# Two joined transformer blocks with routed experts: group and experts chosen in common steps, attention kinds in one sequence, new norms between the stages

## Chip, cores and metric

One core of one Trainium2 chip runs the whole forward pass in one launch. The metric is the device time of one execution in microseconds; less is better. All data is fp32.

## What is computed

Batch 1, 256 tokens of width 1024. The first block also reads 256 context tokens. It modulates and normalises, projects, and mixes in three ways side by side: differential attention (4 heads over context and own tokens), a gated linear scan in two directions ("GLA"), and neighbourhood attention ("na", 4 heads with a bias); then comes the routed feed-forward. The second block has two layers with latent attention, a stick-breaking mixer and pooling, and a routed feed-forward of the same kind.

```python
x = x + mod[2] * (concat([ya, yb, yn]) @ w_out)          # first block
h2 = rms_norm(x, g2) * (1 + mod[4]) + mod[3]
x = x + mod[5] * hier_moe(h2, ...)
x = rms_norm(x, final_g)                                  # between the blocks
# second block, twice:
x = x + mixed(rms_norm(x, norm1_g)) @ w_out
x = x + hier_moe_2(rms_norm(x, norm2_g), ...)
# hier_moe: argmax of 4 groups, the 2 best of the group's 8 experts,
#   gate = softmax(two logits) * softmax(groups)[group]
#   y[token] += gate * (silu(g) * u) @ w_down[expert],  g, u = split(h[token] @ w_up[expert])
```

Each token goes to 2 of 32 experts. An expert of the first block has 6 MB of weights (up 1024 x 1024, down 512 x 1024), one of the second block 3 MB. All the weights of the 32 experts are loaded in each of the three expert stages.

## The kernel before

The five engines run programs of their own that meet at semaphores; `at(name)` in the code counts what an engine has to wait for. `link` puts an operation of VectorE or ScalarE and a wait for its end in one. SyncE issues all weight loads into a ring of slots in SBUF, in a fixed order. A slot is loaded again when it is given back: the up slots by VectorE (`up_used`, after the product of SiLU and up in an expert's last round), the others by TensorE (`piece_used`).

**Attention of the first block.** `attention_pe`, `attention_act` and `attention_dve` work through items, one for each pair of heads (or head with its two maps) and tile of 128 tokens. An item is: scores on TensorE, row maximum on VectorE, exponential on ScalarE, normalisation on VectorE, transposes on TensorE, their copy on ScalarE, and after two items the values on TensorE and their copy (`outputs`) on VectorE. Scores run two items ahead. The kernel calls them twice, with 4 items of "na" and then 8 of "diff"; each call ends before the next begins. The GLA's norm is worked in between: `ones64` sums squares over 64 partitions and spreads the sums, so mean, reciprocal and root are done on 512 columns.

**Residual and norm.** `out_steps_pe` makes 16 matmuls, 8 for each tile of 128 tokens, and `residual_dve` adds a tile to X after its eighth. ScalarE squares each tile with a sum along the row (`squares_act`), VectorE makes the mean and its reciprocal (`rstd_dve`), ScalarE the root (L804), VectorE the scaled tiles (L820), TensorE turns them, VectorE and ScalarE copy with gain and shift.

**Routing** (`route_pe`, `route_dve`). After the logits VectorE chooses the group in five steps (`first_of`: maximum, equal, number, minimum, equal), takes the group's eight logits, chooses the first expert in five steps and the second in five, and writes `chosen` (L950). TensorE meanwhile does sums of zeros to stay busy (L860), then ranks the tokens of each expert with triangular matmuls (L898 to L902). VectorE marks the tokens of the first round (L1248), TensorE gathers their rows.

**Expert rounds** (`experts_pe`, `experts_act`, `experts_dve`). A round serves up to 32 tokens of one expert (of two experts in the second block): turned rows `got`, up matmuls (L1128 or L1137), SiLU (L1218), product (L1285), turned, down matmuls, copy `y_sb` (L1223), combine with the gates into PSUM (L1115). Beside it the next round's rows are gathered. An expert with more tokens has further rounds; their count is read from memory into a register by each engine (`next_extra`). Before the first round VectorE clears `comb` and `y_sb` and works out the gates (`route_gates_dve`), then `each_round` reads the count and starts.

**Joins.** After the first block the combined sum is multiplied by a gate row and added to X, X is normalised with `final_g` and written (L879), then squared and normalised again for the second block's first norm. At the end GpSimd sends X out in one transfer.

**The order of the loads** (`expert_loads`): the first 6 ring loads of a stage go early, others after the mixers, after the residual, and from then on each as its slot comes free.

## Time and profile before

| | us |
|---|---|
| median of the 3 runs shown | 1614.74 |
| lowest and highest of them | 1606.09, 3355.39 |
| the profiled execution | 1603.31 |
| its span | 1601.4 |
| TensorE busy in the span | 1334.5 (83%) |
| VectorE, ScalarE, GpSimd busy | 441.8, 394.3, 44.7 |
| moved by DMA | 479.78 MB, mean 300 GB/s |

The span goes from the first to the last instruction of the profiled execution; some 2 us lie around it. The stages by the trace: to about 200 us modulation and projections, 200 to 292 the mixers, to 333 projection, norm and routing, 333 to 814 the 32 experts of the first block, then a layer to 1197, whose experts begin at 967, and a layer to 1601, whose experts begin at 1343.

### The profile page before, as it was taken

The numbers are of one execution on the slowest core, as the hardware profiler recorded it, in microseconds if no ns is written. First come the engines' busy times: TensorE is split into PE (matmuls) and PEld (weight loads), VectorE is DVE, ScalarE is ACT, GpSimd is POOL, SyncE is SP. The second block draws the span as 40 slices with busy tenths as digits, with TensorE's granted clock in tenths as the row PEclk, the third lists the DMA queues.
The fourth block names the chain that finished last, engine by engine and source line by source line (L and its number), as shares of the span: only waits on it lengthen the run. The fifth ranks groups of instructions, "written<-read, shape, count | busy, mean of one in ns | idle before, by whom it ended". The sixth has DMA issues, their size and how long they took to land.

```text
span 1601.4 us, 31814 instructions
## 1 busy us (share of the span) xinstructions
PE 1334.5 (83%) x12448; PEld 692.8 (43%) x12449; DVE 441.8 (28%) x1332; ACT 394.3 (25%) x766; POOL 44.7 (3%) x68
## 2 busy tenths in 40 slices
PE   4999976988666776699989898987899898999975
PEld 3555443444232332355546543433337544434332
DVE  2004366432111121122233533111122534221212
ACT  2101235122111121122223322222132322222212
POOL 2000210000000000000000000000000000000000
PEclk9999989999899999999999999999899999999987
DMA  9959302769999999989773286999992344689994
GB/s 365 376 208 286 101 9 92 264 240 410 410 410 410 409 410 410 410 357 410 307 288 147 91 309 242 418 417 417 419 381 96 142 147 182 240 321 418 418 417 181
DMA packets 120161, 479.78 MB, mean 300 GB/s; under 512 B 9185, under 2 KB 19774, under 8 KB 103406
## 3 DMA queue, kind: packets, MB, share of 16 engines
q1 hardware_dynamic: 116352, 468.61, 74.4%
q0 software_dynamic: 2848, 8.86, 1.8%
q10 hardware_dynamic: 910, 1.59, 0.3%
q8 instruction: 37, 0.61, 0.2%
q14 instruction: 14, 0.11, 0.0%
HBM read 477.05 MB, written 1.97 MB: 299 GB/s over the span
## 4 chain that ended last, share of the span: by engine, by line
PE 57%; SPq 19%; DMA 9%; DVE 7%; issue 4%; ACT 2%; ACTq 0%; DVEq 0%; POOL 0%; PEldq 0%
SPq L512 19%; PE psum L1137 6%; PE psum L1857 6%; DMA store<-in_w_up 6%; PE psum L761 5%; PE psum L1115 5%; PE psum L1088 5%; PE psum L1128 5%; PE psum L1148 3%; PE psum L1155 2%; PE psum L1853 2%; DMA store<-in_w_expert_up 2%; PE psum L1402 2%; PE psum L1390 2%; PE psum L1435 1%
## 5 line engine op out<-in xcount | busy, mean ns | idle before, releaser
L1128 PE MATMUL psum<-store 128*32 128x256 f32 x2624 | 172.5, 403 | 71.8 <-DMA store<-in_w_expert_up 70.6
L1137 PE MATMUL psum<-store 128*32 128x256 f32 x2432 | 156.4, 414 | 25.1 <-DMA store<-in_w_up 23.1
L1285 DVE TENSOR_TENSOR store<-store,psum 128x128 f32<-128x128 f32 x79 | 22.7, 288 | 528.1 <-ACT store L1218 527.0
L1128 PEld LDWEIGHTS psum<-store 128*32 128x32 f32 x2624 | 78.1, 113 | 150.5 <-DMA store<-in_w_expert_up 99.8
L1088 PE MATMUL psum<-xn,store 128*32 128x256 f32 (+1 forms) x992 | 126.8, 478 | 5.7 <-DVE store L1248 5.7
L1115 PE MATMUL psum<-store 32*128 32x256 f32 (+1 forms) x992 | 127.6, 469 | 1.9 <-ACT store L1223 1.9
L1137 PEld LDWEIGHTS psum<-store 128*32 128x32 f32 x2432 | 88.5, 119 | 83.2 <-issue 34.3
L1218 ACT ACT_TABLE_LOAD x79 | 101.4, 1283 | 49.0 <-issue 48.8
L1218 ACT ACTIVATE store<-psum 128x128 f32<-128x128 f32 x79 | 21.9, 277 | 315.2 <-PE psum L1128 186.7
L1857 PE MATMUL psum<-store 128*128 128x512 f32 x224 | 97.7, 593 | 0.0
L1115 PEld LDWEIGHTS psum<-store 32*128 32x128 f32 (+1 forms) x992 | 57.9, 184 | 73.2 <-issue 68.0
L1155 PE MATMUL psum<-store 128*32 128x256 f32 x1312 | 81.0, 383 | 10.1 <-DMA store<-in_w_expert_down 3.2
L761 PE MATMUL psum<-store 128*128 128x512 f32 x192 | 87.2, 601 | 2.3 <-DVE store L738 2.0
L1292 DVE COPY store<-psum 128x256 f32<-128x256 f32 x79 | 33.5, 424 | 179.4 <-ACT store L1221 179.4
L1223 ACT ACTIVATE store<-psum 128x256 f32<-128x256 f32 (+1 forms) x79 | 38.4, 486 | 170.8 <-PE psum L1155 89.9
L1148 PE MATMUL psum<-store 128*32 128x512 f32 x608 | 73.1, 597 | 2.1
L1106 PE MATMUL psum<-const_sb,store 128*128 128x128 f32 x158 | 32.8, 290 | 47.6 <-PE psum L1155 17.9
L1088 PEld LDWEIGHTS psum<-xn,store 128*32 128x32 f32 (+1 forms) x992 | 43.1, 127 | 66.5 <-issue 45.6
L1212 ACT ACTIVATE store<-psum 128x256 f32<-128x256 f32 (+1 forms) x82 | 40.0, 488 | 108.6 <-PE psum L1088 108.6
L1857 PEld LDWEIGHTS psum<-store 128*128 128x128 f32 x224 | 41.9, 190 | 49.9 <-issue 49.7
L1106 PEld LDWEIGHTS psum<-const_sb,store 128*128 128x128 f32 x158 | 15.8, 140 | 98.5 <-issue 98.5
L1155 PEld LDWEIGHTS psum<-store 128*32 128x32 f32 x1312 | 37.8, 109 | 43.3 <-ACT store L1221 11.6
(331 smaller groups left out, 1440.0 us busy)
## 6 DMA issues: line engine op xcount, KB each, us to landing
store<-in_w_expert_up SPq DMA_DIRECT2D x128, 1024.0 KB, 18.2
store<-in_w_expert_down SPq DMA_DIRECT2D x64, 1024.0 KB, 18.3
store<-in_w_gate SPq DMA_DIRECT2D x64, 1024.0 KB, 17.8
store<-in_w_up SPq DMA_DIRECT2D x64, 1024.0 KB, 19.8
store<-in_w_down SPq DMA_DIRECT2D x64, 1024.0 KB, 20.2
store<-in_w_mod SPq DMA_DIRECT2D x12, 2048.0 KB, 14.4
store<-in_w_in SPq DMA_DIRECT2D x6, 2048.0 KB, 12.7
store<-in_w_out SPq DMA_DIRECT2D x6, 2048.0 KB, 15.1
```

The source lines that it names most:

```text
L512: sp.dma_start(dst, src).then_inc(sems[f"piece{slot}"], 16)
L761: mm = pe.matmul(ps[2 * t + n], mixT[:, 4 * j + k, P * t:P * t + P], w[:, k, 512 * n:512 * n + 512], start=(j == 1 and k == 0), stop=(j == ...
L1088: mm = pe.matmul(G[w * j:w * j + w, 0:wide], sel[:, t, 0:w], xn[:, t, wide * j:wide * j + wide], start=(t == 0), stop=(t == NT - 1))
L1106: mm = pe.transpose(U[:, S + P * t:S + P * t + P], sel_gate[:, t, :], ident)
L1115: mm = pe.matmul(out_, comb[r, P * t:P * t + P], y_sb[r, 0:S * at_once], start=False, stop=True, skip_group_check=True)
L1128: mm = pe.matmul(out_(j), chosen_rows(k, 0), wt[:, kk, :, j, :], start=(k == 0), stop=(k == KD - 1))
L1137: mm = pe.matmul(out_(j), chosen_rows(k, e), wt, start=(k == 0), stop=(k == KD - 1))
L1148: mm = pe.matmul(Y[quadrant(j), :], hidT[:, W * src:W * src + W], pair[e][:, half, 512 * n:512 * n + 512], start=(half == 0), stop=(half = ...
L1155: mm = pe.matmul(Y[quadrant(j), 0:S], hidT[:, W * k:W * k + W], wt[:, kk, S * j:S * j + S], start=(k == 0), stop=(k == 3))
L1212: act.activation(raw[:, 0:wide], G[:, 0:wide], ACT.Copy).then_inc(sems["w_raw"], 1)
L1218: act.activation(silu_sb, U[:, 0:P], ACT.Silu).then_inc(sems["w_silu"], 1)
L1857: mm = pe.matmul(bank, hT[:, k, P * i:P * i + P], w[:, k, :], start=(k == 0), stop=(k == KD - 1))
```

## The change

- "na" and "diff" items form one sequence of 12; the queue of each engine runs through it without an end in between. `outputs` of a group comes before the maximum of the item after next. The GLA's norm works on 8 columns and is spread by eight matmuls with the identity.
- The last tile of the projection is released by TensorE in halves and added in halves.
- Router logits of groups and experts lie side by side in five sets of eight (4 groups filled up with a large negative number, 4 x 8 experts). The maximum and first place of all five are found in the same five steps, the second places of the four sets of experts in five more, and the group's marks pick the result. Differences and exponentials of the gates are made after `chosen`.
- VectorE waits for `ranked` and reads its first count before the first gather.
- The expert up weights of the first block are read with row 8p + k on partition p instead of 128k + p; norm, gains, shift and router weights follow (two modulation rows go through DRAM to get this order).
- The gate row of the first block is multiplied into `y_sb` by VectorE in each round, in place of ScalarE's copy and of the product at the join.
- `join_act` and `join_dve`: both norms between the blocks from one root of four columns: the second sum of squares is taken on X times gain and scaled afterwards. X itself is written later.
- A root of one column (`root_ahead_act`) ahead of each wait for the sums.
- The last combine of a layer signals after its first tile. SyncE sends the output tile by tile.

```diff
-            up = ins["w_expert_up"][0].rearrange("e (k p) n -> e p k n", p=P)
+            up = ins["w_expert_up"][0].rearrange("e (p k) n -> e p k n", p=P)
...
-                if step % 8 == 7:
+                if step in (7, 11, 15):
                     mm.then_inc(sems["out_mm"], 1)
...
+                if done == "out_mm" and t == NT - 1:
+                    for n in range(2):
+                        if n:
+                            dve.wait_ge(*at(done))
+                        half, src = slice(512 * n, 512 * n + 512), ps[bank + 2 * t + n]
+                        if gate is not None:
+                            link(dve.tensor_tensor(res_tmp[:, half], src, gate[:, half], ALU.mult))
+                            src = res_tmp[:, half]
+                        ins_ = dve.tensor_tensor(X[:, t, half], X[:, t, half], src, ALU.add)
+                    ins_.then_inc(sems["resid"], 1)
...
+        def root_ahead_act(act):
+
+            act.activation(cols[:, 88:89], ones[:, 0:1], ACT.Sqrt)
+
+        def join_act(act, at):
+
+            root_ahead_act(act)
+            for t in range(NT):
+                act.wait_ge(*at("resid"))
+                ins_ = act.activation(junk_of(t), X[:, t, :], ACT.Square, accum_out=ss[:, t:t + 1])
+            ins_.then_inc(sems["sumsq"], 1)
+            act.wait_ge(*at("sumsq"))
+            for t in range(NT):
+                act.wait_ge(*at("xg"))
+                ins_ = act.activation(junk_of(t), xn[:, t, :], ACT.Square, accum_out=ss[:, NT + t:NT + t + 1])
+            ins_.then_inc(sems["sumsq"], 1)
+            act.wait_ge(*at("sumsq"))
+            act.wait_ge(*at("mean"))
+            act.activation(rstd, ss, ACT.Sqrt).then_inc(sems["sqrt_done"], 1)
...
+        def join_dve(dve, at, link):
+
+            for t in range(NT):
+                dve.tensor_tensor(xn[:, t, :], X[:, t, :], final_g, ALU.mult).then_inc(sems["xg"], 1)
+            first, second = ss[:, 0:NT], ss[:, NT:2 * NT]
+            dve.wait_ge(*at("sumsq"))
+            link(dve.tensor_scalar(first, first, 1.0 / D, EPS, ALU.mult, ALU.add))
+            link(dve.reciprocal(first, first))
+            dve.wait_ge(*at("sumsq"))
+            link(dve.tensor_tensor(second, second, first, ALU.mult))
+            link(dve.tensor_scalar(second, second, 1.0 / D, EPS, ALU.mult, ALU.add))
+            dve.reciprocal(second, second).then_inc(sems["mean"], 1)
+            dve.wait_ge(*at("sqrt_done"))
+            link(dve.tensor_tensor(rstd[:, NT:2 * NT], rstd[:, NT:2 * NT], rstd[:, 0:NT], ALU.mult))
...
-            for _ in range(2):
-                idle_sum_pe(pe, 2)
-                pe.wait_ge(*at("lg"))
+            idle_sum_pe(pe, 3)
...
+            first_of(lg5, 1 + NG, top5, mark5, first5)
+            link(dve.scalar_tensor_tensor(rest4, first5[:, :, 1:, :], -BIG, lg5[:, :, 1:, :], ALU.mult, ALU.add))
+            first_of(rest4, NG, top4, mark4, second4)
+            link(dve.tensor_tensor(rest4, first5[:, :, 1:, :], second4, ALU.add))
+            dve.tensor_tensor(chosen.rearrange("p t (g e) -> p t g e", g=NG), rest4, group_marks(), ALU.mult)\
+                .then_inc(sems["route"], 1)
...
+                if which == 1:
+                    dve.wait_ge(sems["w_y"], v)
+                    dve.tensor_tensor(y_sb[:, 0:S], Y[:, 0:S], gate_y, ALU.mult).then_inc(sems["w_ysb"], 1)
...
             extra_rounds_dve(dve, at, link, which)
+            first_extra(dve, "dve", at)
             v = dve.snap(win)
             gathered(v + (part + 1))
             dve.memset(comb, 0.0).then_inc(sems["w_comb_sb"], 1)
-            dve.memset(y_sb, 0.0).then_inc(sems["w_ysb"], 1)
+            dve.memset(y_sb[:, 0:S * at_once], 0.0).then_inc(sems["w_ysb"], 1)
+            if which == 1:
+                dve.wait_ge(sems["gate_moe_in"], 64)
...
+            for t in range(NT):
+                sp.wait_ge(sems["fin_x"], NT + t + 1)
+                sp.dma_start(out[0, P * t:P * t + P, :], X[:, t, :]).then_inc(sems["written"], 16)
...
-            for dram, part in zip(gates_dram, (2, 5)):
+            for dram, part in zip(gates_dram, (2, 5, 4, 3)):
...
+            pool.wait_ge(*at("logits"))
+            for n in range(4):
+                pool.dma_start(gate_y[W * n:W * n + W, :], gates_dram[1][S * n:S * n + S].rearrange("(o n) -> o n", o=1)
+                               .to_broadcast([W, S])).then_inc(sems["gate_moe_in"], 16)
...
-            attention_pe(pe, at, "na", between_na)
-            attention_pe(pe, at, "diff")
+            attention_pe(pe, at, ("na", "diff"), between_na)
...
-                    link(dve.tensor_scalar(gl_s, psum[:, 6:8, S:2 * S], 1.0 / 64, EPS, ALU.mult, ALU.add))
-                    dve.reciprocal(gl_s, gl_s).then_inc(sems["gla_mean"], 1)
...
+                    link(dve.tensor_scalar(gl_r, ps[6][:, S:S + 8], 1.0 / 64, EPS, ALU.mult, ALU.add))
+                    dve.reciprocal(gl_r, gl_r).then_inc(sems["gla_mean"], 1)
+                if i == 3:
+                    dve.wait_ge(*at("gla_b"))
```

## Rows read from the trace of the kernel before

**Rows 1.** Windows: stretch, its length, busy us per engine, clock, DMA share, GB/s
```profile
64.00:69.00 5.00, 4.78 (x54) 2.74 (x46) 0.33 (x2) 0.56 (x2) 0.00 (x0) 1.00 1.02 404
324.00:328.00 4.00, 4.00 (x6) 1.52 (x5) 2.54 (x16) 0.20 (x1) 0.00 (x0) 0.59 0.41 165
332.00:336.00 4.00, 3.03 (x52) 1.76 (x55) 3.15 (x15) 1.28 (x1) 0.00 (x0) 1.00 0.00 0
440.00:530.00 90.00, 58.45 (x794) 26.76 (x786) 14.12 (x54) 15.62 (x30) 0.00 (x0) 0.94 1.03 410
672.00:812.00 140.00, 131.45 (x2074) 73.44 (x2078) 37.01 (x141) 40.00 (x78) 0.00 (x0) 0.99 0.92 362
1010.00:1050.00 40.00, 36.27 (x375) 16.05 (x379) 8.34 (x29) 11.25 (x18) 0.00 (x0) 1.00 1.02 417
```

**Rows 2.** Waits from 333 to 560 us, and from 672 to 812
```profile
PEld psum L1128 <- DMA store<-in_w_expert_up: 61.3, 38, 2.0
...
PEld psum L1128 <- DMA store<-in_w_expert_up: 2.0, 1, 2.0
```

**Rows 3.** Windows of the attention (PE, PEld, DVE, ACT, POOL), and its timeline
```profile
226.05:277.20 51.15, 33.19 (x144) 19.75 (x144) 32.60 (x65) 22.85 (x52) 0.58 (x1) 0.87 0.20 72
231.00:243.73 12.73, 10.83 (x54) 7.09 (x56) 1.87 (x7) 5.37 (x7) 0.58 (x1) 0.84 0.00 0
...
226.77 3.35 DVE L2305 RECIPROCAL store<-store 128x512 f32<-128x512 f32 x1
...
241.00 1.28 ACT L673 ACT_TABLE_LOAD   x1
...
276.78 0.42 DVE L738 COPY xn<-psum 128x256 f32<-128x256 f32 x1 [2.69 <-PE psum L638]
```

**Rows 4.** Timeline, residual and norm: start, us, engine, line, what, idle before
```profile
215.06 0.70 DVE L709 TENSOR_TENSOR psum<-psum,store 128x512 f32<-128x512 f32 x1
...
308.51 1.22 DVE L791 TENSOR_TENSOR store<-psum,store 128x1024 f32<-128x1024 f32 x1 [4.36 <-PE psum L761]
...
946.78 2.22 DVE L820 TENSOR_SCALAR xn<-X,small 128x1024 f32<-128x1024 f32 x2 [1.61 <-ACT small L804]
```

**Rows 5.** Timeline, first stage's routing
```profile
322.10 0.23 DVE L929 TENSOR_TENSOR store<-psum,small 128x72 f32<-128x72 f32 x1 [5.04 <-PE psum L889]
...
326.69 0.29 DVE L950 TENSOR_TENSOR store<-store 128x32 f32<-128x32 f32 x2
...
328.05 0.30 PE L898 MATMUL psum<-store,const_sb 128*128 128x32 f32 x2
...
329.61 0.20 DVE L963 TENSOR_SCALAR store<-store 128x64 f32<-128x64 f32 x1
```

**Rows 6.** Timeline, first round of the first and of the second stage
```profile
338.46 0.17 DVE L1278 COPY store<-store 128x4 f32 x1 [1.60 <-issue]
...
339.53 0.29 DVE L1285 TENSOR_TENSOR store<-store,psum 128x128 f32<-128x128 f32 x1 [0.57 <-issue]
339.60 0.37 SPq L512 DMA_DIRECT2D store<-in_w_expert_up  x1
...
971.85 0.17 DVE L1278 COPY store<-store 128x8 f32 x1 [1.33 <-issue]
```

**Rows 7.** Timeline, join of the two blocks
```profile
814.21 1.23 DVE L791 TENSOR_TENSOR store<-psum,store 128x1024 f32<-128x1024 f32 x1 [2.54 <-PE psum L1115]
...
820.98 1.28 ACT L804 ACT_TABLE_LOAD   x1 [0.59 <-DVE small L809]
...
826.67 0.20 ACT L804 ACTIVATE small<-small 128x2 f32<-128x2 f32 x1 [0.49 <-DVE small L809]
826.91 1.42 DVE L820 TENSOR_SCALAR xn<-X,small 128x1024 f32<-128x1024 f32 x2 [0.33 <-ACT small L804]
```

**Rows 8.** Timeline, last combine of a layer and the output
```profile
1193.36 1.99 PE L1115 MATMUL psum<-store 64*128 64x512 f32 x8 [0.72 <-ACT store L1223]
...
1593.28 0.72 POOL L1372 DMA_DIRECT2D out<-X  x1 [233.68 <-DVEq L882]
```

More of the change, by code:

```diff
@@ L563, in second_sources, with items_of @@
             return [gate[0], up[0], gate[1], up[1], down[0], down[1]]
-        def items_of(kind):
-            return [(g, t) for g in range(2 if kind == "na" else 4) for t in range(NT)]
+        def items_of(kinds):
+            return [(kind, g, t) for kind in kinds for g in range(2 if kind == "na" else 4) for t in range(NT)]
         def keys_of(kind, t):
@@ L585, in values_of, with attention_pe @@
             return ps[7][:, S * (g % 2):S * (g % 2) + S] if kind == "mla" else ps[6 + g % 2][:, 0:S]
-        def attention_pe(pe, at, kind, between=None, fill=None):
-            items = items_of(kind)
+        def attention_pe(pe, at, kinds, between=None, fill=None):
+            items = items_of(kinds)
             def scores(i):
-                g, t = items[i]
+                kind, g, t = items[i]
                 if i >= 2:
@@ L733, in normalise, with outputs @@
                 ins_.then_inc(sems["probs"], 1)
-            def outputs(g):
-                dve.wait_ge(*at.plus("pv", g + 1))
+            def outputs(group):
+                kind, g, _ = items[NT * group]
+                dve.wait_ge(*at.plus("pv", group + 1))
                 dst = oA[:, g, :] if kind == "diff" else mix_of(kind)[:, (6 if kind == "na" else 0) + g, :]
-                dve.tensor_copy(dst, values_of(kind, g)).then_inc(sems["pv_sb"], 1)
+                dve.tensor_copy(dst, values_of(kind, group)).then_inc(sems["pv_sb"], 1)
             maxima(0)
@@ L745, in attention_dve @@
                 normalise(i)
+                if i % NT == NT - 1 and i >= NT:
+                    outputs(i // NT - 1)
                 if i + 2 < len(items):
@@ L776, in out_rest_pe, with residual_dve @@
             out_free_pe(pe, at)
-        def residual_dve(dve, at, link, bank, done, gate=None, quarters=False):
+        def residual_dve(dve, at, link, bank, done, gate=None, quarters=False, first=None):
             if done == "out_mm":
-                at(done, 2)
+                at(done, 3)
             for t in range(NT):
-                if done == "out_mm" or t == 0:
+                if first and t == 0:
+                    dve.wait_ge(*at(first))
+                elif first or done == "out_mm" or t == 0:
                     dve.wait_ge(*at(done))
@@ L1201, in experts_pe @@
             pe.wait_ge(sems["w_comb_sb"], v + (part + 1))
-            combine().then_inc(sems["moe_mm"], 1)
+            combine("moe_first" if which == 2 else None).then_inc(sems["moe_mm"], 1)
         def experts_act(act, at, which, part):
@@ L1370, in second_block_pool @@
                 .then_inc(sems["final_gain"], 16)
-            pool.wait_ge(*at("fin_x"))
-            pool.dma_start(out[0].rearrange("(t p) d -> p t d", p=P), X).then_inc(sems["written"], 16)
-            pool.wait_ge(sems["written"], 16)
         def second_block_pe(pe, at, plan, piece_ready):
             for layer in range(2):
-                steps = (2, 2, 2, 1) if layer == 0 else (1, 2)
                 idle_pe(pe, 2 - layer)
-                for n in steps:
+                for n in (2 - layer, 2):
                     pe.wait_ge(*at("resid"))
                     idle_pe(pe, n)
+                for _ in range(NT if layer == 0 else 0):
+                    pe.wait_ge(*at("xg"))
+                    idle_pe(pe, 1)
                 norm_pe(pe, at, lambda n: idle_pe(pe, n, bank=0))
```

278 lines of the change are left out of this document (151 added, 127 removed).

## The prediction

> **What bounds the kernel now.** I read first the windows by stretch, since the three expert stages are most of the time. In 440 to 530 us, inside the first one, the DMA engines are full at 410 GB/s and TensorE is busy two thirds of the time; in 1010 to 1050, inside the second, they move 417 GB/s [rows 1]. Then the waits: up to 560 us TensorE's weight loads stand 38 times behind the up weights, from 672 us to the stage's end once [rows 2]. So in the first stage the loads decide until about 672 us, and after that TensorE's own rounds do (131.45 of 140 us busy, DMA share 0.92 [rows 1]), because several late experts need further rounds with the same weights. Ahead of the loads stands a serial piece: at 332 to 336 us nothing is moved at all [rows 1], for every ring slot is full until VectorE ends the first round's product at 339.82 and the next load is issued [rows 6]. What shortens the serial chain before that point shifts the whole stage; what happens beside the full DMA is hidden. The other serial pieces are the attention of the first block, the norms and routing ahead of each stage, and the joins after each.
>
> **The change, part by part.** All is summed against the profiled execution: span 1601.4, its own time 1603.3 us.
>
> Attention, windowed and differential in one sequence. From 226.05 to 277.20 VectorE is busy 32.60 of 51.15 us and TensorE 33.19; between 231 and 243.73, where the first kind drains and the second fills, VectorE does 1.87 us in 12.73 [rows 3]. The GLA norm puts a 3.35 us reciprocal before the third item's normalisation; with 8 columns steps of 0.17 replace it and its forerunner of the same width. I laid the three queues out from the durations of these rows and their neighbours: third normalisation at 226.5 instead of 230.0; the first differential maximum at 227.6 instead of 243.7; there is one new wait of VectorE for TensorE's values of the first group (1.5 us), one for the broadcast of the root by TensorE (1.2 us, eight small matmuls, queued on TensorE ahead of the next scores), and ScalarE loads the root's table and the exponential's again between two exponentials instead of in the gap, 1.28 us each [rows 3]. From the sixth item on VectorE sets a pace of 6.9 us per group of two, and the last copy ends at 266.5 instead of 277.20: 10.7, of which I take 10.5. Floor of the gain 5 (the reciprocal and two us of the drain, if TensorE's values block the scores at a low clock); ceiling 15: TensorE's 33.19 plus 1.5 for the broadcasts, begun at 227.5, end at 262.2.
>
> Last residual tile in halves. VectorE's first operation on the last tile starts at 308.51, when TensorE is done, and takes 1.22; a 512-wide one takes 0.70 [rows 4]. Every add waits there, since a tile was released whole. Of two 1.22 operations two of 0.70 are left behind TensorE in the first block: 1.0. In each later layer one of each: 0.5. Together 2.0; between 1 and 2.5.
>
> Strided norm in the first block. Two tiles scaled with plain rows take 1.42 [rows 7], by partition 2.22 [rows 4]. Cost 0.8. The router's loads become runs of eight rows, off the path. The two new transfers of the modulation columns and the two that bring them back are queued on GpSimd with over 30 us of slack before anyone waits.
>
> Routing. Selection runs from 322.10 to 326.98 [rows 5], 4.9 us in some 20 steps on 4 to 32 columns, 0.2 us apart. Now there are five steps on 80 columns, five on 64, and four more. A 64-column step takes 0.20 [rows 5] and 0.03 to the next; I take 0.25 for 80: 0.12 + 0.25 + 5 x 0.25 + 5 x 0.23 + 3 x 0.23 = 3.45, a gain of 1.4. In the first stage TensorE's first rank matmul came at 328.05 [rows 5], 1.1 us after the selection, behind four filler sums at a granted clock of 0.59 [rows 1]; there are three now, which keeps pace: 1.3. Three stages: 4.1; between 2.5 and 6. What is moved behind the selection (0.9 us) hides beside TensorE's ranking.
>
> Head of the expert stage. Before its first-round copy VectorE stands 1.60 us in the first stage and 1.33 in the second, the read of the count [rows 6]. Without a read the engine's turn costs 0.57 [rows 6], so 1.0 and 0.8 go. The read now lies before the first gather, where VectorE waits for TensorE: in the first stage 0.2 sticks out. The shorter gate chain gives 0.25, the smaller clearing 0.25. ScalarE's SiLU is not what the product at 339.53 waits for: the idle time before it is put to issue, not to ScalarE, and I take it that this slack is enough. So 1.3, 1.0 and 1.0: 3.3. In the first stage the gate rows are four transfers that GpSimd issues after the logits, and VectorE waits for them some 7 us later with the issue of the first rounds' loads queued behind its product; if they land late that costs up to 1.5, which I put into the range only. The gate's product at each round's end replaces a copy of ScalarE and lies beside TensorE's next up matmuls.
>
> Loads of the first stage. The up weights are now read as runs of 8 KB instead of 4. The second block's stages have just this mix (8 KB for gate and up, 4 for down) and move 417 to 418 against 410 GB/s [rows 1]. Over the 327 us from 345 to 672 this is 327 x (1 - 410/418) = 6.3; I take 6.5. Floor 0. After 672 it gives nothing.
>
> Join of the blocks. From VectorE's first operation at 814.21 to the end of the scaled tiles at 826.91 + 1.42 = 828.33 it takes 14.1 [rows 7]. Now: two adds without a gate (2.5), two gain products (2.5, the squares beside them), the last square (1.25), three small steps (0.6), one root (0.25), one step and two scalings (1.65): 8.8. Gain 5.3, one table load among it. The final gain on X moves behind the turning, beside TensorE's next projection.
>
> The root's table ahead. The load of 1.28 stands between VectorE's small steps and the root [rows 7]; where none is needed the root takes 0.20 [rows 7]. Besides the join's it goes at four places (both layers' second norms, the second layer's first, the end), and ScalarE is idle for over a microsecond before each: 4 x 1.3 = 5.2; floor 0, if the loads are placed where they were. The Trainium skill, ScalarE: Activation LUTs, section What ACT_TABLE_LOAD costs, counts a drain besides, about 2.66 us for a switch. By that the five loads would give 6.9 us more and the time would be about 1560; here the root starts 1.30 us after the load's start, so the trace shows no drain.
>
> First tile of the last combine. It takes 1.99 us [rows 8]; VectorE can now start after its first half: 1.0 at each of two ends, 2.0. The output goes out by SyncE in two transfers, the last half as large, without GpSimd's issue of 0.72, 8.1 us before the span's end [rows 8]: 1.2, between 0 and 2.5. One more small transfer and 72 more constant columns at the start: cost 0.3, up to 1.
>
> Sum: 10.5 + 2.0 - 0.8 + 4.1 + 3.3 + 6.5 + 5.3 + 5.2 + 2.0 + 1.2 - 0.3 = 39.0. That gives 1564.3 for a profiled execution. The unprofiled runs shown are 1606.1 and 1614.7 (the third, 3355, is an outlier), 3 to 11 above the profiled one; I add 3 and forecast **1567**.
>
> **Rivals.** (1) The attention stays in step: TensorE's values of the old kind stand before the scores, VectorE's outputs wait for them ahead of the next maximum, and the clock falls (mean 0.87 there [rows 3]). Gain 5 instead of 10.5: 1572. Against it: VectorE had 10.9 us of free time in the drain alone [rows 3]. (2) The norms and loads do not pay: the tables are loaded where they were (5.2) and the rate stays at 410 (6.5): 1579. (3) Gains ahead of the stages are absorbed, because the first loads and not VectorE's product decide when the ring moves: head and routing (7.4) and half of the attention gone, 1580. Against: the DMA idles at 332 to 336. (4) The other side: the runs of 8 KB at a pitch of 32 KB between partitions are slower than the unbroken megabyte. Slower than before from a rate of 373 GB/s down: then the 327 us grow by 32, which eats the other 32. For it: nothing in the trace has this pitch. Against: the modulation weights are 4 KB runs at a pitch of 24 KB and still move 404 [rows 1]. At 330 GB/s the stage up to 672 takes 79 more and the rest, which moves 51 MB in 140 us now, some of it for the next stage [rows 1], would need up to 154: at least 1603 - 32 + 79 = 1650, and 3 = 1653. [...]
>
> **How the numbers follow.** The forecast gets 0.60, rival 1 0.14, rival 2 0.12, rival 3 0.09, rival 4 0.05. A measurement of this kernel can tell about 2 per cent, 32 us, from no change, so faster by that means below some 1574 to 1582. The forecast lies just beyond it and takes most of its 0.60, rival 1 two thirds: 0.64 faster. Rivals 2 and 3 and the rest are within: 0.30. Slower 0.06. The range: the bounds of the parts, not all at one end, give a gain of 28 to 48, and the runs lie 3 to 11 above the profiled time: 1556 to 1590.
>
> **What would show it.** Right: VectorE's reciprocal of 3.35 gone and the last attention copy some 10 to 11 us earlier; windows of the first stage at 417 GB/s; no table load at the root's line; the first load after the routing about 13 us earlier; a single root of four columns at the join. Wrong: a stretch of idle VectorE between the kinds of attention, a rate below 410, or a wait of VectorE before the gates' steps.

## The result, and the profile after

| | us |
|---|---|
| median of the kernel after, 4 runs (lowest, highest) | 1565.84 (1562.64, 1566.82) |
| median of the kernel before beside them, 4 runs (lowest, highest) | 1610.41 (1606.05, 3355.39) |
| ratio without the run of 3355 us, 95% interval | 0.9729 (0.9687 to 0.9770) |
| the same in the later run after_again, 5 runs | 1565.55; 0.9714 (0.9695 to 0.9732) |
| profiled execution after, its span | 1566.48, 1564.7 |

The change makes the kernel 2.7 per cent faster in the first comparison and 2.9 in the second (the intervals together: 2.3 to 3.1). Two runs far above their fellows, 3355.39 us of the kernel before and 1787.72 us of count_late below (granted clock 0.742, the others 0.95 or more), are left out of every ratio. Windows of the first expert stage, after: length, busy us of each engine, granted clock, DMA share, GB/s.

```profile
350.00:450.00 100.00, 76.39 (x1079) 37.57 (x1071) 22.22 (x80) 17.86 (x33) 0.00 (x0) 0.93 1.02 418
...
672.00:790.00 118.00, 110.35 (x1767) 61.99 (x1769) 36.76 (x134) 28.87 (x52) 0.00 (x0) 1.00 0.89 356
```

The rate is up from the 410 of [rows 1], and the last part is TensorE's as before (busy 110.35 of 118 us). Timeline of the attention after (answers to [rows 3]):

```profile
231.22 0.20 DVE L2401 RECIPROCAL small<-small 128x8 f32<-128x8 f32 x1
...
232.62 1.28 ACT L2169 ACT_TABLE_LOAD   x1
...
235.11 1.28 ACT L681 ACT_TABLE_LOAD   x1
236.35 0.42 DVE L751 COPY store<-psum 128x256 f32<-128x256 f32 x1 [1.66 <-PE psum L646]
...
239.47 0.75 DVE L2404 SCALAR_TENSOR_TENSOR store<-store,small,psum 128x512 f32<-128x512 f32 x1 [0.62 <-PE psum L2013]
...
270.69 0.42 DVE L751 COPY xn<-psum 128x256 f32<-128x256 f32 x1 [2.69 <-PE psum L646]
```

The 3.35 us reciprocal is 0.20 now, the root's table is loaded between exponentials, and the two new waits, for TensorE's values and for the broadcast, cost 1.66 and 0.62: I had 1.5 and 1.2. The last attention copy ends at 271.11 instead of 277.20, although this execution began its mixers 5 us later. Selection and the ranking behind it, after ([rows 5]):

```profile
314.82 0.17 DVE L1004 TENSOR_TENSOR store<-psum,small 128x8 f32<-128x8 f32 x1 [4.37 <-PE psum L966]
...
315.42 0.24 DVE L994 TENSOR_TENSOR store<-store 128x80 f32<-128x80 f32 x1
...
318.32 0.23 DVE L1010 TENSOR_TENSOR store<-store 128x64 f32<-128x64 f32 x1
...
318.90 0.30 PE L973 MATMUL psum<-store,const_sb 128*128 128x32 f32 x2
```

It takes 3.73 us where it took 4.88, and TensorE's ranking starts 0.35 behind it in place of 1.1. The head of the first stage ([rows 6]):

```profile
324.54 5.35 PE L1190 MATMUL psum<-store 128*32 128x256 f32 x64 [1.28 <-DVE store L1333]
...
327.95 0.17 DVE L1341 COPY store<-store 128x4 f32 x1 [0.57 <-DVE store L1321]
...
329.95 0.28 ACT L1280 ACTIVATE store<-psum 128x128 f32<-128x128 f32 x1 [4.98 <-PE psum L1190]
330.26 0.29 DVE L1348 TENSOR_TENSOR store<-store,psum 128x128 f32<-128x128 f32 x1 [1.81 <-ACT store L1280]
330.32 0.34 SPq L518 DMA_DIRECT2D store<-in_w_expert_up  x1
```

VectorE's 1.60 before its copy is gone, but it now stands 1.81 for ScalarE's SiLU, which stands for TensorE's up matmuls: 5.35 us at a granted clock of 0.65 (324 to 328 us), where the kernel before took 3.66 at 1.00. The first load is issued at 330.32, 9.3 us earlier than before (339.60 [rows 6]); I had written about 13, and most of the difference is the start, 5 us later in this execution. The join ([rows 7]) and the last combine with the output ([rows 8]):

```profile
798.06 2.47 DVE L820 TENSOR_TENSOR X<-X,psum 128x1024 f32<-128x1024 f32 x2 [1.30 <-PE psum L1175]
...
804.87 0.20 ACT L842 ACTIVATE small<-small 128x4 f32<-128x4 f32 x1 [0.76 <-DVE small L871]
805.31 1.42 DVE L876 TENSOR_SCALAR xn<-xn,small 128x1024 f32<-128x1024 f32 x2
...
1554.52 2.48 DVE L820 TENSOR_TENSOR X<-X,psum 128x1024 f32<-128x1024 f32 x2 [2.82 <-PE psum L1175]
...
1559.02 2.48 DVE L882 SCALAR_TENSOR_TENSOR X<-X,small,store 128x1024 f32<-128x1024 f32 x2 [0.33 <-ACT small L852]
1560.34 1.56 SPq L1756 DMA_DIRECT2D out<-X  x2
```

From the first add to the scaled tiles the join takes 8.7 (806.73 less 798.06; forecast 8.8, before 14.1), with one root of four columns and no load before it. The output now leaves 1.3 us behind the start of VectorE's last pair of products.

**The same stretches in all traces.** One pair of profiled executions can't show terms of 1 us, so I cut every trace at the same marks: first bias add, end of the last attention copy, end of the first round's product, first add of the join, start of the second norm's scaling, first product, last add, and so on. Means in us. Left out are the stretches where the experiment's own edit or its other data act, and down_8k altogether; of the two kernels whose data differ, no expert stage behind the join but the last is used.

| stretch | before (executions) | after and its variants | gain | forecast |
|---|---|---|---|---|
| start to bias add | 216.5 (3: 215.1 to 217.9) | 217.8 (8: 215.6 to 220.1) | -1.3 | -0.3 |
| attention | 63.9 (3: 62.1 to 64.7) | 51.6 (9: 50.0 to 53.9) | 12.2 | 10.5 |
| projection to the first product | 62.7 (3) | 59.5 (9: 58.0 to 61.1) | 3.2 | 2.8 |
| first stage to the join | 474.3 (2) | 468.4 (7: 467.5 to 469.8) | 5.9 | 6.5 |
| join, first layer's mixer, to the norm | 132.6 (3) | 126.5 (9: 123.8 to 128.5) | 6.1 | 7.1 |
| first layer: norm to product | 26.4 (3) | 25.3 (9: 24.5 to 26.3) | 1.1 | 2.4 |
| its stage | 222.2 (2) | 221.3 (7) | 0.9 | 1.0 |
| second layer's mixer, to the norm | 126.2 (3: 124.1 to 127.3) | 124.2 (9: 122.4 to 125.4) | 2.0 | 3.1 |
| second layer: norm to product | 25.6 (3) | 24.1 (9: 23.7 to 25.2) | 1.5 | 2.4 |
| its stage | 237.1 (3: 236.2 to 238.7) | 235.7 (8: 235.0 to 237.9) | 1.4 | 1.0 |
| last add to the end of the span | 16.7 (3) | 10.1 (8) | 6.6 | 2.5 |

The forecasts of this column are its terms put to their stretches; they add up to 39.0, the gains to 39.6. The medians of the unprofiled runs are 45 apart. The profiled execution of before was an early one: 1603.31, while none of the 39 runs of it beside the experiments was under 1606.0 and their medians were 1609.9 to 1610.5. So most of the 5 us between are before's executions and not a part of the change that the rows missed. One trace of a usual length bears on where they lie: before_start, below, took 1609.79 us, 6.5 more than the profiled execution of before, and it spends 1.4 of them at the start, 2.6 in the attention and 2.4 in the last expert stage. That these are the stretches of every usual execution isn't shown.

### The profile page after: what moved, and what is told of

Its sections match the earlier page's. It is cut to its first block, busy times and chain, and to the rows that moved or that the text cites. A ratio compares the mean times of both kernels' runs of the same rounds, so it can differ in the third digit from the quotient of the medians.

```text
span 1564.7 us, 31839 instructions
## 1 busy us (share of the span) xinstructions
PE 1338.8 (86%) x12460; PEld 697.1 (45%) x12461; DVE 454.9 (29%) x1358; ACT 379.1 (24%) x730; POOL 47.8 (3%) x74
## 3 DMA queue, kind: packets, MB, share of 16 engines
q0 software_dynamic: 2688, 7.43, 1.7%
q10 hardware_dynamic: 1054, 1.63, 0.3%
## 4 chain that ended last, share of the span: by engine, by line
PE 58%; SPq 18%; DMA 12%; DVE 6%; issue 4%; ACT 2%; ACTq 0%; DVEq 0%; PEldq 0%
SPq L518 18%; PE psum L1199 6%; PE psum L1938 6%; DMA store<-in_w_up 6%; PE psum L774 5%; PE psum L1190 5%; PE psum L1175 5%; PE psum L1148 4%; DMA store<-in_w_expert_up 4%; PE psum L1210 3%; PE psum L1934 3%; PE psum L1217 2%; PE psum L1470 2%; PE psum L1458 2%; PE psum L1503 1%
## 5 line engine op out<-in xcount | busy, mean ns | idle before, releaser
L1190 PE MATMUL psum<-store 128*32 128x256 f32 x2624 | 176.7, 411 | 58.9 <-DMA store<-in_w_expert_up 57.5
L1148 PE MATMUL psum<-xn,store 128*32 128x256 f32 (+1 forms) x992 | 130.0, 490 | 1.3 <-DVE store L1311 1.2
L1274 ACT ACTIVATE store<-psum 128x256 f32<-128x256 f32 (+1 forms) x82 | 40.0, 487 | 104.0 <-PE psum L1148 104.0
L1938 PEld LDWEIGHTS psum<-store 128*128 128x128 f32 x224 | 41.9, 190 | 49.9 <-issue 49.7
L774 PEld LDWEIGHTS psum<-store 128*128 128x128 f32 x192 | 36.0, 193 | 41.6 <-issue 41.3
## 6 DMA issues: line engine op xcount, KB each, us to landing
store<-in_w_in SPq DMA_DIRECT2D x6, 2048.0 KB, 12.2
```

What stands on the lines that cost most here:

```text
L774: mm = pe.matmul(ps[2 * t + n], mixT[:, 4 * j + k, P * t:P * t + P], w[:, k, 512 * n:512 * n + 512], start=(j == 1 and k == 0), stop=(j == ...
L1148: mm = pe.matmul(G[w * j:w * j + w, 0:wide], sel[:, t, 0:w], xn[:, t, wide * j:wide * j + wide], start=(t == 0), stop=(t == NT - 1))
L1190: mm = pe.matmul(out_(j), chosen_rows(k, 0), wt[:, kk, :, j, :], start=(k == 0), stop=(k == KD - 1))
L1938: mm = pe.matmul(bank, hT[:, k, P * i:P * i + P], w[:, k, :], start=(k == 0), stop=(k == KD - 1))
```

## The experiments

The start. **start_late**, against the kernel after:

```diff
-            act.dma_start(norm2_pk, ...norm2_g...).then_inc(sems["params"], 16)      # in the first wait
+                pool.dma_start(norm2_pk, ...norm2_g...).then_inc(sems["rows_pk"], 16)
```

> The kernel after, with one edit: the 1024 gains of norm2_g go to SBUF by GpSimd together with the two modulation rows, late, instead of by ScalarE ahead of the first wait for the parameters. In the kernel after VectorE's first residual-like add of the mixers (the bias add) begins at 220.11 us, before at 215.06: 5.05 us that the forecast had at 0.3. Theory A: the added transfer delays the parameters by 0.6 us, this moves TensorE's first work, and TensorE then runs 30 to 50 us at half clock while the loads wait for it. Then the add is back at 215 to 216 here, the granted clock in 30 to 35 us back at 1.0, and the time 4 to 5 us shorter, about 1561. Rival B: the loss comes from the 72 further constant columns or from a clock that falls as it likes in each execution: the add stays at 219 to 221 and the time within 1 us of 1566.

Measured: 1563.98 (1561.24 to 1570.03, 5 runs), ratio 0.9705 (0.9687 to 0.9724); TensorE's first wait 12.9 against 13.3 us, the bias add at 218.72. **before_start** is the kernel before with the same transfer in the first wait and 80 columns:

> The kernel before, with only the additions at the start: the transfer of norm2_g in the first wait and 80 instead of 8 columns of the number row. Theory A: the bias add moves from 215.06 to about 220 and the time goes up by 4 to 5 us. Rival B (chance of the clock): both within 1 us of before. The forecast's own term was 0.3.

Measured: 1610.51 (1604.97 to 1618.16, 12 runs), 1.0005 of before (0.9991 to 1.0019); first wait 13.2 us against 12.7, bias add at 216.47. And **after_again**, the kernel after unchanged:

> The kernel after unchanged, as the base for differences of a few us. Theory A (the clock's falls are chance, since the kernel before with the additions at the start timed 1.0005 of before): the bias add begins anywhere from 215 to 221 us, the time is 1562 to 1570 with a median of 1565. Rival: the late start is fixed to this program: 220 us again.

Measured: 1565.55, bias add at 217.93, so 220 is not fixed to the program. Theory A of the first two falls: with the addition the start is anywhere from 215.6 to 220.1, and before did not get slower by it. The addition does move TensorE's first wait by 0.5 us. What the late starts have in common is the clock. Windows of the kernel after, then of start_late:

```profile
30.00:35.00 5.00, 2.28 (x44) 2.12 (x48) 0.00 (x0) 0.27 (x1) 0.00 (x0) 0.67 1.08 354
...
40.00:45.00 5.00, 3.70 (x17) 3.33 (x16) 2.75 (x6) 2.84 (x6) 5.00 (x10) 0.50 1.01 327
```

```profile
30.00:35.00 5.00, 2.70 (x57) 2.70 (x61) 0.00 (x0) 0.28 (x1) 0.00 (x0) 0.76 1.08 351
...
40.00:45.00 5.00, 3.70 (x14) 2.97 (x13) 1.84 (x4) 2.25 (x4) 4.98 (x9) 0.50 1.01 319
```

TensorE is busy 2.3 to 2.7 of the 5 us in the first stretch and 3.7 in the second, and both executions have the lower clock, 0.50 (1.2 GHz), in the second; before had 0.94 there. Over all 14 traces the order is clean: the five with 0.50 or 0.51 from 40 to 45 us (after, start_late, no_root_ahead, out_gpsimd, down_pairs_lean) begin the bias add at 218.2 to 220.1, the nine with 0.74 to 0.94 at 215.1 to 217.9. None of the three traces with before's code is among the five; with three traces that doesn't tell whether the change makes the low clock likelier. One program can have either level elsewhere, too. One stretch of the first layer's mixer in the kernel after, then in after_again:

```profile
862.00:867.00 5.00, 4.61 (x7) 2.40 (x8) 0.13 (x1) 0.00 (x0) 0.00 (x0) 0.50 0.00 0
```

```profile
862.00:867.00 5.00, 3.76 (x11) 2.20 (x12) 1.89 (x7) 0.00 (x0) 0.00 (x0) 1.00 0.00 0
```

With 4.3 us between the two in the whole stretch from join to norm (128.10 and 123.78) for identical code, a loss of 2 to 3 us of a mixer in one trace can't be put down to an edit.

**no_root_ahead**, the kernel after with the two calls of `root_ahead_act(act)` removed:

> The kernel after without the root of one column ahead of the sums. The forecast: five loads of the root's table of 1.28 us return to the path (join, both layers' second norms, the second layer's first, the end): plus 6.5, about 1572, and ScalarE's load at the root's line right ahead of the root, VectorE waiting 1.61 us there instead of 0.33. Rival 1: a drain comes with each load, as the Trainium skill, ScalarE: Activation LUTs, What ACT_TABLE_LOAD costs, has it (about 2.66 us for a switch): plus 13, about 1579. Rival 2: the load hides beside something else: within 1 us of 1566.

Measured: 1574.95 (1571.93 to 1579.82), ratio 0.9780 (0.9758 to 0.9801), 9 us over the kernel after; by the spread of the runs it could be 6 as well as 15, so the time alone leaves rival 1 (a drain with each load, plus 13) open. The rows decide. Timeline of the first layer's second norm:

```profile
926.58 1.28 ACT L850 ACT_TABLE_LOAD   x1 [0.55 <-DVE small L855]
927.87 0.20 ACT L850 ACTIVATE small<-small 128x2 f32<-128x2 f32 x1
928.11 2.23 DVE L891 TENSOR_SCALAR xn<-X,small 128x1024 f32<-128x1024 f32 x2 [1.61 <-ACT small L850]
```

The root starts 1.29 to 1.30 us after the load does, at all five places. VectorE waits 1.61 us in place of 0.33 at four of them, and the join takes 9.9 in place of 8.7: 1.28 each, 6.4 in all. The term stands, and rivals 1 and 2 fall. The rest lies in the mixers: without their two loads each they take 128.4 and 125.8 us, at the long end of the table's spread (to 128.5 and 125.4) or just beyond it. The clock is the likely cause; it isn't shown.

**out_gpsimd**, the kernel after with the output by GpSimd in one transfer after both products:

> The kernel after, with the output sent as before: one transfer of both tiles by GpSimd after the last product. The forecast counted 1.2 us for this change. By the two traces 8.5 us lie between VectorE's last product and the span's end before and 3.2 after. Theory A: the whole difference belongs to the path of the transfer: plus 5 us, about 1571, with 8 us from the last product to the span's end. Rival: only 1.2 belongs to it and the rest to where the last product's halves ended: about 1567.

Measured: 1570.52 (1567.46 to 1571.90, 5 runs), ratio 0.9745 (0.9726 to 0.9764). Its end:

```profile
1557.40 2.48 DVE L882 SCALAR_TENSOR_TENSOR X<-X,small,store 128x1024 f32<-128x1024 f32 x2 [0.33 <-ACT small L852]
1560.17 0.72 POOL L1441 DMA_DIRECT2D out<-X  x1 [231.59 <-DVE X L882]
```

The span ends at 1568.5, 7.6 us after GpSimd's issue is done. In the kernel after it ends 2.8 us after SyncE's second issue is done (1561.90 to 1564.7). From the last add the end takes 15.6 here and 10.15 there: theory A, 5.4 us. The edit changes the queue and the splitting into two transfers together, so how the 5.4 divides between them is not shown.

**attention_apart**, the kernel after with one line changed to two for each engine:

```diff
-            attention_pe(pe, at, ("na", "diff"), between_na)
+            attention_pe(pe, at, ("na",), between_na)     # TensorE waits for gla_y once, before
+            attention_pe(pe, at, ("diff",))               # the last values of "na"
```

> The kernel after with the two kinds of attention as two sequences again, as before, but with the GLA norm on 8 columns kept; TensorE waits besides for the GLA product before the windowed kind's last values, 1 to 2 us in the drain. The stretch from the normalisation of the third item to the last attention copy was 11.1 us shorter after than before. The forecast laid out the join of the queues as the larger part: reciprocal and its forerunner 3.35 + 0.68 less 0.36, so 3.7, and 7.4 from the overlap of drain and fill. Theory A: plus 7.4 and 0 to 2 for the added wait: 1573 to 1575. Rival (the reciprocal was what held the drain; overlap gives little): plus 2 at most, 1567.

Measured: 1571.10 (1564.55 to 1575.59, 5 runs), ratio 0.9746 (0.9721 to 0.9772), 5.5 over the kernel after; the attention stretch 57.95 against 51.6: 6.3. Its drain:

```profile
228.37 0.88 DVE L744 TENSOR_SCALAR store<-store,small 128x512 f32<-128x512 f32 x2
233.49 0.42 DVE L751 COPY store<-psum 128x256 f32<-128x256 f32 x1 [4.24 <-PE psum L646]
235.55 0.75 DVE L2407 SCALAR_TENSOR_TENSOR store<-store,small,psum 128x512 f32<-128x512 f32 x1 [1.63 <-PE psum L2013]
...
239.97 0.42 DVE L751 COPY store<-psum 128x256 f32<-128x256 f32 x1 [2.95 <-PE psum L646]
...
241.71 1.23 DVE L727 TENSOR_REDUCE small<-psum 128x2 f32<-128x1024 f32 x1 [1.31 <-PE psum L610]
```

VectorE waits 4.24, 1.63, 2.95 and 1.31 us between the last normalisation and the first differential maximum. The rival (only the reciprocal counted) falls, and theory A had 7.4 or more, so it is somewhat too high. Of 12.2 us in the attention about half is the overlap, the added wait included. The other half is what is left: the short GLA steps, for which the forecast had 3.7, and what the clock gave (0.82 to 0.84 from 222 to 262 us before; after, 1.00 but for one stretch of 0.83). It wasn't tried by itself, and executions of the same stretch differ by up to 4 us.

**count_late**, the kernel after with `first_extra(dve, "dve", at)` removed and the count read by `each_round` again:

> The kernel after with VectorE's first read of the round count back behind the gates. The forecast's term: 1.0, 1.0 and 0.8 less 0.2 in three stages, plus 2.6, about 1568. Rival, from the trace after, where the first product ends 0.3 us behind ScalarE's SiLU and in the first stage VectorE stands 1.81 us for it: ScalarE is last and the read hides in the first stage; plus 1.0 to 1.5 in all. Both are near what can be timed; the idle time before the first product in the trace decides.

Measured: 1567.58 (1565.22 to 1572.72, 5 runs). The ratio is 0.9737 (0.9715 to 0.9759): not told apart from the kernel after by time. Its first stage:

```profile
320.14 3.66 PE L1190 MATMUL psum<-store 128*32 128x256 f32 x64 [0.97 <-DVE store L1333]
...
323.87 0.28 ACT L1280 ACTIVATE store<-psum 128x128 f32<-128x128 f32 x1 [2.98 <-PE psum L1190]
324.57 0.17 DVE L1341 COPY store<-store 128x4 f32 x1 [1.59 <-issue]
...
325.64 0.29 DVE L1348 TENSOR_TENSOR store<-store,psum 128x128 f32<-128x128 f32 x1 [0.57 <-issue]
```

The 1.59 is back, yet gathered rows to product take 5.85 us here (320.08 to 325.93) and 6.07 in the kernel after (324.48 to 330.55): at a full clock the up matmuls take 3.66 and SiLU is done before VectorE comes; at the low clock of the kernel after and of after_again they take 5.35, and SiLU comes last. One trace, out_gpsimd, reads the count ahead and had the full clock:

```profile
323.65 3.66 PE L1190 MATMUL psum<-store 128*32 128x256 f32 x64 [1.28 <-DVE store L1333]
...
328.13 0.29 DVE L1348 TENSOR_TENSOR store<-store,psum 128x128 f32<-128x128 f32 x1 [0.56 <-ACT store L1280]
```

There the distance is 4.83. From gathered rows to product, in the three stages:

| | first | first layer | second layer |
|---|---|---|---|
| before | 6.50 | 6.20 | 5.11 |
| count_late | 5.85 | 5.82 | 4.73 |
| after, full clock | 4.83 (out_gpsimd) | 5.13 | 4.38 |
| after, low clock | 6.07 | | |

So the read is worth 1.0, 0.7 and 0.35 us where the clock is up, and nothing in the first stage where it is down: the rival's mechanism, and with 1.05 in all its size. The low clock there is no rare event: of the nine traces that read the count ahead and have contiguous columns or every second one, eight have 5.35 to 5.47 us for these matmuls, and out_gpsimd alone has 3.66; the three traces with before's code and count_late all have 3.66. TensorE waits 1.28 us for the gathered rows with the read ahead of them and 0.97 without, but out_gpsimd has the 1.28 too, so what brings the clock down is not shown.

**The loads.** **before_8k** is the kernel before and **after_4k** the kernel after, each with the one line of the change's diff that sets the up weights' layout swapped; each was executed once.

> The kernel before with only the expert up weights of the first block read in runs of 8 KB (row 8p + k). The rest of the layout is left as it was, so the products use rows in a wrong order, and the routing of the second block differs: only the first stage is read, from the first product to the join (474.39 us before). Theory A: the rate goes from 410 to 417 to 418 GB/s and the stage is 6.5 us shorter, 468. Rival: the run length has no part in it, and what made the stage of the kernel after 5 to 7 us shorter was the gate's product in place of ScalarE's copy: 474 again.

> The kernel after with only the runs of the up weights back at 4 KB (rows in a wrong order for the products, as told for the run above; only the first stage is read). Theory A: 410 GB/s and 474 to 475 us from the first product to the join instead of 467.5 to 469. Rival: 468 again, the gain being the round's own.

Windows of before_8k, then of after_4k:

```profile
450.00:550.00 100.00, 70.40 (x891) 32.13 (x883) 15.79 (x60) 17.58 (x33) 0.00 (x0) 0.88 1.02 418
```

```profile
450.00:550.00 100.00, 70.29 (x915) 33.80 (x911) 18.74 (x67) 14.89 (x26) 0.00 (x0) 0.89 1.03 410
```

Product to join: 467.47 with 8 KB runs in the kernel before (474.39 with 4), 476.15 with 4 KB in the kernel after (467.5 to 469.8 with 8). The layout alone makes the whole gain of the stage, 6.9 and some 7.8 us; both rivals fall. With equal runs the stage with the new rounds is 1 to 2 us longer than with the old (476.15 to 474.3, 468.4 to 467.5). Candidates are the gate's product per round and a small part of the earlier start absorbed by the loads; neither was tried by itself.

**down_8k** and **down_pairs** take it further. Down rows 4p + k (2p + k in the second block) on partition p, and up columns to match; then in pairs:

```diff
-            down = ins["w_expert_down"][0].rearrange("e (k p) n -> e p k n", p=P)
+            down = ins["w_expert_down"][0].rearrange("e (p k) n -> e p k n", p=P)           # down_8k
+            down = ins["w_expert_down"][0].rearrange("e (i p r) n -> i e p r n", i=2, p=P)  # down_pairs
...
-                               chosen_rows(k, 0), wt[:, kk, :, j, :]        # k u q n
+                               chosen_rows(k, 0), wt[:, kk, :, :, j]        # k u n q: every 4th column
+                               chosen_rows(k, 0), wt[:, kk, :, j // 2, :, j % 2]   # k u i n r: every 2nd
...
-                            wt = pair_of(i, e)[:, :, S * k + P * half:S * k + P * half + P]
+                            wt = pair_of(i, e)[:, :, S * k + half:S * k + S:2]     # both kernels
```

> The kernel after, with the down weights of all three stages also read in runs of 8 KB (row 4p + k, in the second block 2p + k, on partition p); the up matmuls take every fourth (second) column as moving data to match. Theory A (run length sets the rate, two thirds of the bytes brought 410 to 418): the rest brings 422 or so in the first stage's windows, 1 per cent of some 700 us bound by loads: minus 5 to 8, 1558 to 1560. Rival 1: the rate stays at 418, nothing changes. Rival 2: the strided columns slow TensorE's up matmuls (3.66 us for 64 of 128x256 now): slower by 32 rounds and more in the part that TensorE bounds.

> The kernel after with the down weights of all stages in runs of 8 KB, but by pairs of rows (256i + 2p + r), so that the up matmuls take every second column and not every fourth. In the run with every fourth column a matmul of the first stage went from 411 to 632 ns, with every second in the second block from 408 to 411, while the rate rose to 422 GB/s. Theory A: rate 422 and matmuls at 410 ns in all stages: minus 3 in the first stage (327 us bound by loads), minus 1 to 2 in each later one, about 1559 to 1561. Rival 1: the second block's stages are bound by TensorE's rounds nearly as much as by loads, so only the first stage gains: 1562. Rival 2: stride two costs in the first stage too: slower than 1566.

The groups of the costliest up matmuls: of the kernel after, of down_8k, of down_pairs.

```profile
L1190 PE MATMUL psum<-store 128*32 128x256 f32 x2624 | 176.7, 411 | 58.9 <-DMA store<-in_w_expert_up 57.5 <-DVE store L1333 1.3
L1199 PE MATMUL psum<-store 128*32 128x256 f32 x2432 | 156.4, 414 | 25.0 <-DMA store<-in_w_up 23.1 <-DVE store L1330 1.6
```

```profile
L1190 PE MATMUL psum<-store 128*32 128x256 f32 x2624 | 306.5, 632 | 1.8 <-DVE store L1333 1.3 <-DMA store<-in_w_expert_up 0.5
L1199 PE MATMUL psum<-store 128*32 128x256 f32 x2432 | 156.7, 411 | 24.2 <-DMA store<-in_w_up 22.4 <-DVE store L1330 1.6
```

```profile
L1190 PE MATMUL psum<-store 128*32 128x256 f32 x2624 | 184.4, 421 | 54.4 <-DMA store<-in_w_expert_up 53.1 <-DVE store L1333 1.3
```

Windows of down_pairs:

```profile
450.00:550.00 100.00, 73.61 (x951) 33.21 (x947) 19.45 (x70) 15.54 (x28) 0.00 (x0) 0.88 1.01 422
```

down_8k: 1621.16 (1619.34 to 1643.51, 8 runs), ratio 1.0087 (1.0052 to 1.0123), 55 us over the kernel after. The rate is 422, and every fourth column takes 632 ns for 411; the stage is 523.5 us, bound by TensorE throughout (it waits 0.5 us in all for up weights). The mean of one matmul understates it, since they overlap: 64 of them in a row take 3.66 us contiguous and 7.48 with every fourth column, twice as long, and in its first round 7.43 at a granted clock of 0.76 to 0.82, so there the time hardly follows the clock. Rival 2 holds.

down_pairs: 1562.04 (1557.94 to 1563.61, 5 runs), ratio 0.9695 (0.9668 to 0.9721). Its first stage takes 467.97, no less than after: 422 for 418 over 320 us is 3.0, and against it the matmuls take 7.7 us more over 41 rounds (184.4 less 176.7; a group of 64 takes 3.83 to 3.85 for 3.66 at the full clock), of which those behind the hand-over at some 670 us lie on the path. In the second block, too, a group of 64 takes 3.83 to 3.85 for 3.66; the means of one hide this (414 ns after, 406 in down_pairs), presumably because they mix stretches of both clock levels. The last layer's stage takes 235.16 (235.1 after). The first layer's takes 218.99, and down_pairs_lean, with the same stage, has 221.73 (after: 221.2). So the cost of rival 2 is there, about as large as the gain in rate. Its median is the lowest measured here, but its interval overlaps that of the kernel after. **down_pairs_lean**:

> The same as the run before, and the transfers of both blocks' second gains (norm2_g and norm2_g_2) taken out of the first wait and given to GpSimd later. Theory A: TensorE's first wait ends 0.5 to 1 us earlier (12.9 us with one of them moved, 13.3 with both there), and with the clock's chance this is minus 1 to 2: about 1558 to 1560. Rival: the loads of the modulation weights set the start, nothing changes against the run before.

Measured: 1563.53 (1559.14 to 1566.23, 5 runs), ratio 0.9699 (0.9672 to 0.9727). The first wait ends at 12.70 us against 13.11 in down_pairs, but the bias add comes at 218.24 against 216.12, so nothing is won at the start. That the loads of the modulation weights set it, as the rival has it, is not shown.

## Why the prediction was right

The time, 1565.8 and 1565.6, is 1 us beside the forecast of 1567, and the main terms (attention, rate of the loads, join, root's table) are what I said they are. That the number is so close is partly luck, twice over. The gain is 45 between the medians where I summed 39, and before's own median is 1610, 4 above the 1606 that my "add 3" assumed. And within the table's 39.6 for 39.0, 4.1 us too little at the end, 1.7 in the attention and 0.8 in two other rows make up for 6.0 too much in the other seven. The range of 1556 to 1590 is 2 to 4 us wider than its own parts give (1558 to 1586). Point by point:

- Attention: the queues laid out by hand gave 10.5, measured 12.2 as a mean (11.1 in the first pair of traces). Splitting the kinds again costs 6.3 of it, so the overlap is shown; the rest by its size only. Rival 1 would have left half of the gain; it didn't come.
- Halves and strided norm: the scaling takes 2.23 us as counted, and the halves 0.69 each. Projection to the first product gained 3.2 where I had 2.8 in all, which bears the sum, not each term.
- Routing: 3.73 for the selection, I had 3.45, since a step of 80 columns comes every 0.27 us and not every 0.25. The gain is 1.15, not 1.4; the ranking is earlier as forecast.
- Head of the expert stage: the step that failed in its reasoning. "I take it that this slack is enough" was right only in part. Before, the product came 2.14, 1.84 and 0.76 us behind the end of ScalarE's SiLU in the three stages. After, at a full clock, 0.47, 0.77 and 0.03 us of this are left: enough in the first two. In the third stage I took over the second's 1.0, though before's trace has no stand of 1.33 there and only 0.76 of slack; it gained 0.73. In the first stage SiLU comes last at the low clock, and the head gains 0.43 (6.50 to 6.07) instead of 1.3; at the full clock it gains 1.67.
- Norm to product gained 1.1 and 1.5 instead of 2.4 twice, and the head is the smaller part of that (it gave 1.1 and 0.7 for 1.0 twice). From the first step of the selection to the ranks 1.2 and 1.1 are gained. What was lost lies beside them. From the scaling to the first step of the selection the first layer takes 8.7 us before and 9.0 after where the clock stays at 1.00, but 10.2 to 10.5 in the four traces where it falls to 0.50 behind the scaling; and in two traces one gather takes 6.3 for 5.1.
- Loads: 410 to 418 as read from the second block's mix, 5.9 for 6.5, and 6.9 and 7.8 when the line was swapped alone. Rival 4 (the pitch of 32 KB is slow) falls with the 418. The Trainium skill, DMA: Bandwidth & Descriptors, section Latency and other measured facts, has copies at a row pitch of 512 KiB at 207 GB/s and of 4 MiB at 103, for 214 when the pitch of 4 MiB is padded by 4 KiB; 32 KB is below its list, and no run here shows a loss at it.
- Root's table: 1.28 at each of five places by the rows. The Trainium skill, ScalarE: Activation LUTs, section What ACT_TABLE_LOAD costs, has about 2.66 us with a drain for every switch; the rows here show the root 1.29 us after the load's start, so no drain beside the load. ScalarE stood idle ahead of each of these loads. Rival 2 had this and the loads at nothing, and fell in both.
- Join: 14.1 to 8.7, as summed (5.4 for 5.3).
- First tile of the last combine: VectorE's wait before the last add is 2.82 us in both layers where it was 3.67, so 0.85 each for 1.0. The stages gained 0.9 and 1.4.
- Output: the term that was mis-sized most. I counted GpSimd's issue of 0.72 and a half of the transfer, 1.2; the path by GpSimd takes 7.6 us from the issue's end and SyncE's 2.8 from its second one's, and out_gpsimd shows 5.4. The stretch gained 6.6 for 2.5, with 1.3 of it from the root's table.
- Start: -0.3 forecast, -1.3 in the means of a spread of 4.5; before_start and start_late show no cost in the time that can be measured, beside the 0.5 us in TensorE's first wait. In the first comparison the two traces lay 5.05 us apart here, and the later of them is one of the five with the low clock from 40 to 45 us.
- Rival 3 (gains ahead of the stages are absorbed): against it the first product came 9.3 us earlier and the join 16.2, the 6.9 between being the rate's. With runs of 4 KB in both kernels the stage is 1.9 us longer after (476.15 for 474.3), so no more than about that can have been absorbed.

## To carry to other kernels

Where stages hang on one another in a chain, a sum made by rows holds to a few us, and a weak term is one where an engine's idle time is put to "issue": read in each stage by itself what comes next in line, and ask how late it is at the lower clock. Cut several executions at the same marks before a term of 1 to 3 us is explained; the same program differed by 4 us in one stretch. Take the length of the contiguous run of a load into account even at 4 KB, but look at what the new order does to the stride in which TensorE then reads.

## What was not expected of the hardware

- TensorE's moving data in fp32: 64 matmuls of 128x256 in a row take 3.66 us contiguous, 3.83 to 3.85 with every second column and 7.48 with every fourth; the last is 7.43 at a granted clock of 0.76 to 0.82, where contiguous ones at a low clock take 5.35.
- Rate of 1 MB loads: 410 GB/s with runs of 4 KB, 418 with two thirds of the bytes in runs of 8 KB, 422 with all; also at a pitch of 32 KB between partitions.
- With a last transfer of 1 MB by GpSimd the program ends 7.6 us after its issue is done, with the second of two of 0.5 MB by SyncE 2.8 us.
- TensorE's clock at 0.50 or 1.00 in the same 5 us of the same program (862 to 867 us), from one execution to another.
